# First norm of a hybrid block: squares into a buffer of their own, roots two token tiles ahead, gain rows loaded

## The reference, cut to what matters

```python
def rms_norm(x, gain):
    xf = x.astype(jnp.float32)
    y = xf * lax.rsqrt(jnp.mean(xf * xf, axis=-1, keepdims=True) + NORM_EPS) * gain.astype(jnp.float32)
    return y.astype(x.dtype)

h = jnp.concatenate([meta, x], axis=1)
h = h + hybrid_mixer(rms_norm(h, norm_mix[layer]), w_in[layer], ...)
h = h + conv_gated_mlp(rms_norm(h, norm_ffn[layer]), ...)
h = rms_norm(h, norm_final)
```

## Time and profile before

| what | us |
|---|---|
| median of three runs | 1723.76 (1723.76 to 1725.53) |
| profiled execution, its own time | 1719.61 |
| span of the profiled execution | 1717.8 |
| TensorE busy in the span | 1672.9 (97%) |
| VectorE, ScalarE, GpSimd busy | 893.5, 609.6, 485.3 |

### The profile page before, as it was taken

How to read it: one execution, slowest core, us unless ns; L and a number is a source line. 1 busy time by engine, 2 the same in 40 slices (tenths; PEclk the granted TensorE clock), 3 DMA queues, 4 the chain that set the end, 5 groups by cost and what they waited for, 6 DMA issues and landing times.

```text
span 1717.8 us, 30555 instructions
## 1 busy us (share of the span) xinstructions
PE 1672.9 (97%) x12103; PEld 1601.0 (93%) x12103; DVE 893.5 (52%) x969; ACT 609.6 (35%) x990; POOL 485.3 (28%) x471
## 2 busy tenths in 40 slices
PE   7999999998899999999899999999999999999997
PEld 6999999998899999999899998998998999989986
DVE  5566454665444545445542665545545446455457
ACT  6333455535444434434333431221222211212214
POOL 3212212136454334453221132122212211221220
PEclk9999999999999999999999999999999999999999
DMA  5222443246565454553883121111111211211112
GB/s 182 77 92 92 138 140 90 87 116 191 142 169 135 124 143 125 146 156 106 207 268 109 38 62 42 45 47 51 49 37 37 61 49 37 61 40 46 45 40 98
DMA packets 242509, 168.21 MB, mean 98 GB/s; under 512 B 43913, under 2 KB 228840, under 8 KB 241306
## 3 DMA queue, kind: packets, MB, share of 16 engines
q1 hardware_dynamic: 208342, 131.10, 26.7%
q10 hardware_dynamic: 33892, 36.28, 6.4%
q0 software_dynamic: 224, 0.12, 0.0%
HBM read 125.10 MB, written 42.37 MB: 97 GB/s over the span
## 4 chain that ended last, share of the span: by engine, by line
PE 91%; DVE 4%; DMA 2%; ACT 1%; issue 1%; DVEq 1%; POOL 0%; ACTq 0%; SPq 0%
PE gb L842 67%; PE db L1188 11%; PE db L987 4%; PE mb L1188 2%; PE db L900 1%; PE db L1058 1%; PE db L1057 1%; DVE cacc L1694 1%; DMA ot_d<-ots 1%; DVEq L1654 1%; DMA yo<-ot_d 0%; DVE fino L2107 0%; PE db L1128 0%; PE db L1138 0%; PE db L984 0%
## 5 line engine op out<-in xcount | busy, mean ns | idle before, releaser
L842 PE MATMUL gb<-u_hi,w_hi 128*128 128x342 f32 (+2 forms) x2520 | 821.7, 326 | 13.4 <-DVE u_lo L1975 5.7
L842 PE MATMUL gb<-u_lo,w_hi 128*128 128x342 f32 (+2 forms) x2520 | 809.0, 321 | 0.0
L842 PE MATMUL gb<-u_hi,w_lo 128*128 128x342 f32 (+2 forms) x2520 | 806.0, 320 | 0.0
L725 POOL TENSOR_TENSOR w_lo<-w_raw,w_hi 128x1024 fp32r<-128x1024 f32 x130 | 328.9, 2534 | 1043.1 <-ACT w_hi L1232 1043.1
L842 PEld LDWEIGHTS gb<-u_hi,w_hi 128*128 128x128 f32 x2520 | 477.0, 189 | 18.4 <-issue 14.9
L842 PEld LDWEIGHTS gb<-u_lo,w_hi 128*128 128x128 f32 x2520 | 477.3, 189 | 0.4
L842 PEld LDWEIGHTS gb<-u_hi,w_lo 128*128 128x128 f32 x2520 | 476.6, 189 | 0.0
L1232 ACT ACTIVATE w_hi<-w_raw 128x1024 fp32r<-128x1024 f32 x130 | 135.6, 1052 | 7.4 <-ACT tm L1331 5.2
L1694 DVE SCALAR_TENSOR_TENSOR cacc<-xb,prm,cacc 128x1040 f32<-128x1040 f32 x72 | 124.7, 1731 | 10.4 <-issue 8.4
L2072 DVE TENSOR_TENSOR h<-h,db 128x512 f32<-128x512 f32 x138 | 92.5, 684 | 42.2 <-PE db L1188 41.7
L1593 ACT ACTIVATE a_hi<-cv 128x1024 fp32r<-128x1024 f32 x21 | 22.3, 1060 | 247.4 <-PE db L1188 200.5
(11 more groups left out here) (261 smaller groups left out, 1844.0 us busy)
## 6 DMA issues: line engine op xcount, KB each, us to landing
w_raw<-in_w_in SPq DMA_DIRECT2D x53, 512.0 KB, 4.0
w_raw<-in_w_up SPq DMA_DIRECT2D x44, 512.0 KB, 3.8
w_raw<-in_w_down SPq DMA_DIRECT2D x22, 512.0 KB, 3.4
qkT_d<-sl ACTq DMA_DIRECT2D x16, 576.0 KB, 2.8
kv_d<-tm ACTq DMA_DIRECT2D x16, 576.0 KB, 3.4
tk<-kv_d SPq DMA_DIRECT2D x9, 1024.0 KB, 7.6
w_raw<-in_w_out SPq DMA_DIRECT2D x11, 512.0 KB, 8.5
kT<-qkT_d SPq DMA_DIRECT2D x9, 512.0 KB, 5.0
```

Of the source, the lines that this page charges most:

```text
L725: pool.tensor_tensor(lo, w_raw[:, n % SLOTS, :], hi.bitcast(F32), ALU.subtract).then_inc(s_wlo, 1)
L842: mm = pe.matmul(gb[:, bank, 0:w], wt, u, start=(k == 0 and m == 0), stop=(k == KT - 1 and m == 2))
```

## The change

The squares of the first norm are written to cacc instead of xs. With that the wait on s_nt ahead of a root goes, and ACT's order becomes: roots of 0 and 1; then for each j: root of j+2, the two u_hi copies of j, and the w_hi copies as before. The gain is loaded as 16 rows at first (line 491 of before) and as the remaining 112 rows after W_AB, as a DMA that reads the one row 112 times; the copy on ACT goes. The meta tokens are scaled with the 16 loaded rows, ahead of the wait for PE's spread gain; tiles 1 and 2 still read the gain in PSUM, and tiles 3 to 8 the loaded rows.

```diff
             sp.dma_start(xt[0:META, 0, :], meta_tokens).then_inc(s_x[0], 16)
-            sp.dma_start(gmix[0:1, :], norm_mix).then_inc(s_gmix, 16)
+            sp.dma_start(gmix[0:META, :], norm_mix.broadcast_to([META, D])).then_inc(s_gmix, 16)
             sp.dma_start(xt[:, 1, :], x[0, 0:P, :]).then_inc(s_x[1], 16)
             sp.dma_start(cst[:, C_ID:C_ID + P], consts[:, C_ID:C_ID + P]).then_inc(s_const, 16)
             sp.dma_start(xt[:, 2, :], x[0, P:2 * P, :]).then_inc(s_x[2], 16)
             load_w(W_AB, cols(w_in, AB_COL))
+            sp.dma_start(gmix[META:, :], norm_mix.broadcast_to([P - META, D])).then_inc(s_gmr, 16)
...
             def norm_root(j):
                 n = META if j == 0 else P
                 act.wait_ge(s_x[j % 3], 16 * (j // 3 + 1))
-                if j >= 2:
-                    act.wait_ge(s_nt, 2 * (j - 1))
-                root(j, n, xt[0:n, j % 3, :], xs[0:n, j % 2, :], s_nsq)
+                root(j, n, xt[0:n, j % 3, :], cacc[0:n, 0:D], s_nsq)
...
             norm_root(0)
+            norm_root(1)
             for j in range(KT + 1):
-                if j < KT:
-                    norm_root(j + 1)
-                if j == 2:
-                    act.wait_ge(s_xs, 3)
-                    act.activation(gmix[:, :], gb[:, 0:2, :].rearrange("p b c -> p (b c)"), ACT.Copy).then_inc(s_gmc, 1)
+                if j < KT - 1:
+                    norm_root(j + 2)
...
-                gain = gb[0:n, 0:2, :].rearrange("p b c -> p (b c)") if j < 3 else gmix[:, :]
+                gain = gb[0:n, 0:2, :].rearrange("p b c -> p (b c)") if 0 < j < 3 else gmix[0:n, :]
...
+            dve.wait_ge(s_gmix, 16)
+            scale(0)
             dve.wait_ge(s_gmx, 2)
-            scale(0)
             for j in range(KT + 1):
                 if j == 2:
-                    dve.wait_ge(s_gmc, 1)
+                    dve.wait_ge(s_gmr, 16)
```

More of the change, by code:

```diff
@@ L341, in hybrid_block @@
         s_gmx = sem("s_gmx")
-        s_gmc = sem("s_gmc")
+        s_gmr = sem("s_gmr")
         s_uhi = sem("s_uhi")
```

## The result

On the median of ten runs each, the changed kernel takes 1727.24 us (1725.70 to 1731.19) and the kernel before 1723.03 us (1720.63 to 1725.53). The ratio is 1.0023, 95% interval 1.0013 to 1.0034: slower by 4.0 us, 2.2 to 5.9. The forecast was slower by 1.0 us, 1724.8 with a range of 1721.2 to 1727.0, made against a median of 1723.76 for before. The direction and the chain of waits hold; the size is four times what was forecast. The median of 1727.24 is 0.2 us above the range, and 4.0 us are more than the 3.2 that its upper end allowed for the change. Of the timed executions in this document one, of the kernel of experiment 3, took 7321 us and is not counted.

The account below looks back on a forecast made before the run. TensorE, busy 97%, bounds it. Tile 3's landing at 12.3 puts W_AB's high copy at 17.0, turn of tile 4 at 21.7, tile 8 at 34.95: +1.0 us, profiled 1720.6, plus 4.15 for the median, 1724.8; range 1721.2 to 1727.0.

Parts of the forecast that it names:

- high copy of W_AB + 4.69: First norm: TensorE's turn of tile 4 comes 4.69 us after ScalarE starts the high copy of W_AB.
- ScalarE's list: From the root of tile 3: root, pair of u_hi copies, root, pair, 4.74 us to the high copy of W_AB.
- Tile 2: Its load lands at 8.55, so its root starts at 8.7 instead of 9.59, a gain of 0.9 us.
- the landing of tile 3: Load behind the gain rows lands at 12.3, middle of 11.3 and 13.3; this decides, turn of tile 8 = landing + 22.67.
- the upper sum: Tile 3's landing if the slowest DMA engine still has its whole share after W_AB at 10.5: 13.3 us.
- my lower side: Tile 3's landing if all DMA engines go on evenly from about 8.2: 11.3 us, where the change does nothing.
- The first rival: Slowest DMA engine decides: tile 3 at 13.3, +2.0 us, 1725.7; with the slow broadcast 14.6, +3.2, 1727.0. Chance 0.25.
- The stall at tile 7: TensorE's 0.55 us idle before the turn of tile 7, taken as gone: turn of tile 8 at 34.95, otherwise 35.5.
- Roots two ahead: ScalarE's order: root of tile 4 (+1.42) for the gain copy (-0.91) ahead of W_AB's high copy, net +0.5.
- ScalarE's list deciding (faster): Rival: load hidden, tile 3 landing before 11.3; at best -0.8 us, put at -0.5, 1723.3. Chance 0.23.
- The lock going the other way: Rival: scale 4 starts before GpSimd's subtraction of W_AB, which then waits; +0.6 us on top, 1725.4. Chance 0.06.
- Passing the shift on: A shift of the last token turn, that of tile 8, reaches the kernel's end one to one.

Follow-up runs that it names:

- experiment 3: Changed kernel with the gain rows in place but roots one tile ahead, as in the kernel before; ratio to before 1.0007 (0.9997 to 1.0018).
- experiment 5: Changed kernel with the second gain load reading 112 different rows of x instead of one row 112 times; one execution, 1721.82 us.
- experiment 1: Changed kernel without the load of the 112 gain rows, ScalarE copying the gain from PSUM again; ratio to before 1.0008 (0.9999 to 1.0017).
- experiment 4: Kernel before with three unused 128x1024 copies on ScalarE ahead of the high copy of W_AB, a pure delay; ratio to before 1.0030 (1.0020 to 1.0041).
- experiment 8: Experiment 1 with the roots one tile ahead instead of two; ratio to before 0.9991 (0.9982 to 1.0000).
- experiment 9: Experiment 8 with the high copy of the third weight tile made after token tile 4 instead of 5; ratio to before 0.9981 (0.9969 to 0.9992).
- experiment 10: Experiment 9 with no gain copy, tiles 1 to 4 reading PSUM, the 112 rows loaded behind tile 5; ratio to before 0.9988 (0.9979 to 0.9998).
- experiment 11: Kernel before with scales 3 and 4 reading the gain in PSUM, the copy still made; ratio to before 1.0001 (0.9991 to 1.0011).
- experiment 12: Experiment 9 with tiles 3 and 4 reading the gain in PSUM; ratio to before 0.9992 (0.9983 to 1.0001).
- experiment 6: Changed kernel with the 448 KB gain-row load made twice, the second into a buffer not yet in use; one execution, 1726.05 us.
- experiment 2: Changed kernel with the 112 gain rows issued right after the load of tile 3 instead of ahead; ratio to before 1.0020 (1.0011 to 1.0029).
- experiment 7: Experiment 8 with the load of W_AB issued behind that of tile 3; ratio to before 0.9997 (0.9988 to 1.0007).

## Why the prediction was right in its way and too small

- **What bounds it** was right: the difference stands whole at the turn of tile 4, 3.91 us, and comes from what leads to it. The rule "high copy of W_AB + 4.69" gave 24.14; it was 24.13.
- **ScalarE's list** was right to the last digit: 4.74 us from the root of tile 3 to the copy, 14.71 to 19.45.
- **Tile 2** landed at 8.3, the forecast had 8.7; the root of tile 2 gained 1.3 us, which went into waiting for tile 3.
- **The step that failed is the landing of tile 3.** I had 12.3, between 11.3 and 13.3, with 14.6 as the outer bound; it was 14.7 (14.0 and 14.4 in experiments 3 and 5). Against the upper sum, 10.5 + 0.2 + 1.2 + 1.4, two parts were too small. W_AB landed at 11.5 where I had 10.7, and the rows took 1.9 behind it (2.2 in experiments 3 and 5), not 1.2. Tile 3 behind the rows was right, 1.3 for 1.4. With that the even spread over the engines, my lower side, which had pulled the forecast down to the middle, didn't occur. The 1.2 was worked out at the rate at which 512 KB took 1.4 us; at the 248 GB/s that the engines moved from 9 to 13 us 448 KB take 1.85 us, by an estimate. How much of W_AB's lateness is the rows isn't shown: from issue to landing it took 8.4, 7.4 and 7.8 us with the rows behind it (changed, 3, 5), and 6.2 to 7.6 in before and in the seven kernels without (1, 4, 8 to 12). Experiment 5 shows that the rereading isn't the cause, experiments 1, 6 and 10 that the load of the rows at this place is; whether by its bytes or by the slower rate that goes with it stays open.
- **The first rival** (the slowest DMA engine decides) had the right side and a rule, ring order, that doesn't explain the delay of tile 3 by a load behind it in experiment 2. Its price for the landing of 14.6 was +3.2 in the last turn; it was +3.62, with the stall at tile 7 kept.
- **The stall at tile 7** I took as gone. It stayed: the subtraction started at 31.26, the scale at 31.32, and the scale was held. In experiments 1 and 5 the subtraction was held instead, and the stall was gone; in 2 and 6 the scale started 0.05 us ahead as there and was held all the same. I had them within 0.3 us of each other, so which way it went was luck. **From the turn of tile 4 to that of tile 8** it was 13.50, so 12.95 without the stall where I had 13.24: two fewer slow matmuls.
- **Roots two ahead** as an amplifier was in the text ("a late load now stops the ring"), and in the sum it was hidden in the 4.74 from the root of tile 3 to the copy, without a price of its own. Experiments 3 and 8 give it: 2.4 us more from that root to the high copy of W_AB, with a late load and without. As the gain copy (0.91) went at the same time, 1.47 of it shows against the kernel before. With the roots one ahead the late load costs 0.8 us at the turn of tile 4 (experiment 3). Both parts of the change are needed for the result: rows alone +1.5, two ahead alone +1.2, both +3.6 in the last turn, each read from one profile.
- **The other rivals.** ScalarE's list deciding (faster) needed tile 3 before 11.3. Experiment 1 had it at 11.1, but pays the gain copy; the best case as I wrote it, both without a late load and without a copy, was not run with two ahead. The lock going the other way did not occur at tile 4 of the changed kernel. It did in experiment 1, and there the turn of tile 4 came 4.65 us after the high copy of W_AB, no later than by the rule of 4.69, since the scale and the subtraction started together there, where my price had the scale 0.4 us behind.
- **Passing the shift on** one to one: 3.0 of 3.6 at 340 us, 3.7 of 3.9 in experiment 4, and 4.0 (2.2 to 5.9) in the timed runs. Whether the runs hold more than the 3.0 stays open; the interval includes it.
- **The chances.** I had drawn the line of "same" at 3.4 us and gave 0.84 to it, 0.09 to slower by more. The 4.0 lies on the side of the 0.09, the interval on both.

## What to carry to other kernels

Before a copy on an engine is replaced by a load, count the bytes that are in flight at that moment, ahead of *and* behind the load that the engines wait for next: 448 KB put the landing of the next tile from 11.0 to 12.0 us to 14.0 to 14.7 here, and behind tile 5 no token tile was waited for because of them. Asking for data one stage earlier in an in-order engine is worth its load's slack only; where the load can be late, everything queued behind the early request waits with it, and the loss in the last turn was 3.6 us two ahead and 1.5 one ahead. To price an order, count from the landing that starts the list to the instruction that matters (5.66 against 3.28 us here), and not from the last turns alone, where an early landing or a stall that is missing can hide more than half of it. And one profile of each of two kernels doesn't measure a difference of 3 us in a program whose executions differ by 5.

## What of the hardware was not expected

- A load issued 0.4 us behind another on the same queue went with a later landing of the one ahead: 7.1 us for tile 3 in experiment 2, 4.8 to 5.8 in the five kernels without it. For tile 5 in experiment 10 it was 5.5 us against 4.4 to 4.8; in experiment 7, with W_AB behind tile 3, it was 3.7, not longer than before. Each is one execution. The Trainium skill (DMA: Bandwidth & Descriptors, "Queues, rings and completion order") says that each engine takes its descriptors in ring order but that a later one may finish its write first. No run here shows a later load landing first; experiment 2 shows that ring order alone doesn't protect a landing.
- While the gain rows were loaded, repeated or distinct, the DMA engines were busy all the time and moved 248 to 277 GB/s from 9 to 13 us (changed kernel, experiments 3 and 5), against 303 to 327, at a busy share of 0.94 to 1.00, without them (1, 8, 9, 10 and 12).
- VectorE's multiplication with both inputs in SBUF, beside GpSimd's subtraction, ends 1.08 to 1.09 us after the subtraction however early it began: it takes 1.85 us when it began 0.76 before the subtraction's end, 3.23 when 2.14 before, 3.42 when 2.34 before. With one input in PSUM it takes 1.28 (experiment 11), as alone. In experiment 1 the multiplication takes its 1.28 and the subtraction is held, 3.46 instead of 2.35. This agrees with the exclusive lock of the Trainium skill (SBUF — State Buffer, "SBUF: two separate sides"), where the one that starts first holds the ports for its whole instruction. But the recorded starts don't tell which one that is when they are 0.05 us apart, in experiments 1 and 2:

```profile
17.82 1.28 DVE L1662 SCALAR_TENSOR_TENSOR xs<-xt,tiny,gmix 128x1024 f32<-128x1024 f32 x1
17.87 3.46 POOL L725 TENSOR_TENSOR w_lo<-w_raw,w_hi 128x1024 fp32r<-128x1024 f32 x1 [9.89 <-ACT w_hi L1232]
```

```profile
19.75 3.48 DVE L1661 SCALAR_TENSOR_TENSOR xs<-xt,tiny,gmix 128x1024 f32<-128x1024 f32 x1
19.80 2.34 POOL L727 TENSOR_TENSOR w_lo<-w_raw,w_hi 128x1024 fp32r<-128x1024 f32 x1 [11.84 <-ACT w_hi L1234]
```

- The first matmuls after TensorE's idle time start 0.29 us apart and then 0.16. Mostly the granted clock reads 1.00 meanwhile; in experiments 3 and 9 it reads 0.50 over the same steps. How many of the first 11 steps are slow (6 to 11, 4 in experiment 10) changed the way from the turn of tile 4 to that of tile 5 from 4.16 us (experiment 10) to 5.23 (experiment 1); it was 4.39 in the changed kernel.
